# Two interleavings taken out of the compressed attention branch: one product stream after the other, and scores group by group

## What is computed

```
def compress(k, pe, w1, w2):
    blk = k[cmp_idx] + pe[None, :, None, :]
    blk = blk.transpose(0, 2, 1, 3).reshape(n_cmp, G, CMP_BLOCK * dh)
    return jax.nn.silu(blk @ w1) @ w2          # (31, 2, 2048) @ (2048, 256), then @ (256, 64)
k_cmp = compress(kc, pe_k, ck_w1, ck_w2)
v_cmp = compress(vc, pe_v, cv_w1, cv_w2)
sc = jnp.einsum('qghd,cgd->gqhc', qi, k_cmp).astype(jnp.float32) * scale
p_c = jax.nn.softmax(jnp.where(valid[None, :, None, :], sc, NEG), axis=-1)
o_c = jnp.einsum('gqhc,cgd->qghd', p_c.astype(dt), v_cmp)
```

## Time and profile before

| | us |
|---|---|
| median of 3 runs | 2291.12 |
| lowest, highest | 2290.61, 2293.82 |
| the profiled execution (one of the three) | 2293.82 |
| its span in the profile | 2292.0 |
| from the first L1539 to the last VectorE copy of the block | 87.07 to 131.52 |

### The profile page before, as it was taken

One profiled execution on the slowest core, in us unless ns is written; L12 is line 12 of the kernel. 1 busy time (PEld: TensorE's weight loads), 2 busy tenths in 40 slices (PEclk: granted clock), 3 DMA queues, 4 the chain that ended last, 5 costly groups with the idle time before them and its releaser, 6 DMA issues. The chain is left out here.

```text
span 2292.0 us, 26919 instructions
## 1 busy us (share of the span) xinstructions
PE 2137.6 (93%) x10046; PEld 1719.1 (75%) x10046; DVE 1230.9 (54%) x1761; ACT 830.2 (36%) x1204; POOL 18.7 (1%) x46
## 2 busy tenths in 40 slices
PE   7878888999999999998699999999998899999997
PEld 6645666888888888886578888877786577888885
DVE  5576444445443446525567465565535746747465
ACT  4156124433222224224345233343425735424232
POOL 0000000000000000002000000000000000000000
PEclk9889998999999999998799999999999999999998
DMA  4201201322222222221112223221220021232221
GB/s 167 93 1 35 94 28 55 110 101 95 108 92 92 99 96 85 100 89 37 55 61 105 92 94 108 87 97 65 92 94 36 1 88 60 92 111 92 92 96 52
DMA packets 33848, 185.85 MB, mean 81 GB/s; under 512 B 4024, under 2 KB 8280, under 8 KB 14176
## 3 DMA queue, kind: packets, MB, share of 16 engines
q1 hardware_dynamic: 32608, 182.57, 22.7%
q10 hardware_dynamic: 1152, 2.10, 0.3%
HBM read 182.54 MB, written 2.11 MB: 81 GB/s over the span
## 5 line engine op out<-in xcount | busy, mean ns | idle before, releaser
L314 ACT ACTIVATE w_hi<-w_raw 128x2048 fp32r<-128x2048 f32 (+3 forms) x171 | 313.9, 1836 | 846.9 <-PE bank L370 758.8
L368 PE MATMUL bank<-a_hi,w_hi 128*128 128x512 f32 x1488 | 582.8, 392 | 7.0 <-PEq L1442 4.5
L369 PE MATMUL bank<-a_lo,w_hi 128*128 128x512 f32 x1488 | 580.9, 390 | 0.0
L370 PE MATMUL bank<-a_hi,w_lo 128*128 128x512 f32 x1488 | 580.9, 390 | 0.0
L323 DVE TENSOR_TENSOR w_lo<-w_raw,w_hi 128x2048 fp32r<-128x2048 f32 (+3 forms) x171 | 374.8, 2193 | 170.2 <-ACT w_hi L314 170.2
L368 PEld LDWEIGHTS bank<-a_hi,w_hi 128*128 128x128 f32 x1488 | 280.5, 189 | 66.1 <-issue 7.0
L370 PEld LDWEIGHTS bank<-a_hi,w_lo 128*128 128x128 f32 x1488 | 280.4, 188 | 58.7
L369 PEld LDWEIGHTS bank<-a_lo,w_hi 128*128 128x128 f32 x1488 | 280.5, 189 | 57.8
L368 PE MATMUL bank<-big_halves,w_hi 128*128 128x512 f32 x568 | 221.8, 391 | 3.0 <-DVE w_lo L323 3.0
L369 PE MATMUL bank<-big_halves,w_hi 128*128 128x512 f32 x568 | 221.2, 389 | 0.0
L370 PE MATMUL bank<-big_halves,w_lo 128*128 128x512 f32 x568 | 221.1, 389 | 0.0
(11 more groups left out here) (326 smaller groups left out, 2501.0 us busy)
## 6 DMA issues: line engine op xcount, KB each, us to landing
w_raw<-in_w_fu SPq DMA_DIRECT2D x44, 1024.0 KB, 4.8
w_raw<-in_w_up SPq DMA_DIRECT2D x16, 1024.0 KB, 4.8
w_raw<-in_w_down SPq DMA_DIRECT2D x16, 1024.0 KB, 4.8
w_raw<-in_w_fd SPq DMA_DIRECT2D x16, 1024.0 KB, 4.8
w_raw<-in_w_mix SPq DMA_DIRECT2D x8, 1024.0 KB, 4.8
w_raw<-in_w_fd SPq DMA_DIRECT2D x8, 768.0 KB, 4.3
w_raw<-in_w_rqk SPq DMA_DIRECT2D x4, 1024.0 KB, 4.9
w_raw<-in_w_rvg SPq DMA_DIRECT2D x4, 1024.0 KB, 4.8
```

Of the source, the lines that this page charges most:

```text
L314: act.activation(w_hi[slot][:, 0:n], raw[slot][:, 0:n], ACT.Copy).then_inc(hi_ready.sem, 1)
L368: pe.matmul(out, w[0], x[0], start=first, stop=False)
L369: pe.matmul(out, w[0], x[1], start=False, stop=False)
L370: return pe.matmul(out, w[1], x[0], start=False, stop=last)
```

## The change

The lag loop is gone: all 16 matmuls of k (into bank 3) come first, then all 16 of v (into bank 4), both in output partitions 0 to 63, with one signal each. The buffer `hid` becomes 64 partitions by two halves. Silu and the transposes are done once for k and once for v, the transposes with 64 moving columns, into banks 5 and 6. The score loop has the group outermost, and each group's signal comes after its own 16 matmuls. The counts that the engines wait for are moved to fit.

```diff
-            hid = sb(ctx, "cmp_hid", [P, CH])
+            hid = sb(ctx, "cmp_hid", [KV * CB, 2, CH])
...
-                    lag = 6
-                    for n in range(CB // 2 + lag):
-                        for s, j in ((0, n), (1, n - lag)):
-                            if j == 0:
-                                pe.wait_ge(inputs_in[1 + s].sem, loaded[1 + s] + 16)
-                                pe.wait_ge(dve_step.sem, d0 + s + 1)
-                            if 0 <= j < CB // 2:
-                                last = pe.matmul(bank[3][64 * s:64 * s + 64, 0:CH], blk[:, s, j, :, :].rearrange("p g c -> p (g c)"),
-                                                 w1[s][:, j, :], start=j == 0, stop=j == CB // 2 - 1)
-                    last.then_inc(pe_step.sem, 1)
-                    pe.wait_ge(act_step.sem, a0 + 1)
-                    for t in range(2):
-                        last = pe.transpose(bank[5][:, t * P:(t + 1) * P], hid[:, t * P:(t + 1) * P], ident)
-                    last.then_inc(pe_step.sem, 1)
+                    for s in range(2):
+                        pe.wait_ge(inputs_in[1 + s].sem, loaded[1 + s] + 16)
+                        pe.wait_ge(dve_step.sem, d0 + s + 1)
+                        for j in range(CB // 2):
+                            last = pe.matmul(bank[3 + s][0:KV * CB, 0:CH], blk[:, s, j, :, :].rearrange("p g c -> p (g c)"), w1[s][:, j, :],
+                                             start=j == 0, stop=j == CB // 2 - 1)
+                        last.then_inc(pe_step.sem, 1)
+                    for s in range(2):
+                        pe.wait_ge(act_step.sem, a0 + s + 1)
+                        for t in range(2):
+                            last = pe.transpose(bank[5 + s][:, t * 64:(t + 1) * 64], hid[:, s, t * P:(t + 1) * P], ident[0:64, 0:64])
+                        last.then_inc(pe_step.sem, 1)
...
-                    for n in range(4 * TT):
-                        for g in range(KV):
-                            i, h, half = n // 4, n % 4, slice(64 * g, 64 * g + 64)
-                            last = pe.matmul(bank[(2, 7)[g]][:, n * CB:(n + 1) * CB], qk[half, h, i * P:(i + 1) * P], k_cmp[half, :],
-                                             start=True, stop=True)
-                            if n == 4 * TT - 1:
-                                last.then_inc(pe_step.sem, 1)
+                    for g in range(KV):
+                        for i in range(TT):
+                            for h in range(4):
+                                at_col = (i * 4 + h) * CB
+                                last = pe.matmul(bank[(2, 7)[g]][:, at_col:at_col + CB], qk[64 * g:64 * g + 64, h, i * P:(i + 1) * P],
+                                                 k_cmp[64 * g:64 * g + 64, :], start=True, stop=True)
+                        last.then_inc(pe_step.sem, 1)
...
-                    act.wait_ge(pe_step.sem, p0 + 2)
-                    act.activation(hid[:, :], bank[3][:, 0:CH], ACT.Silu).then_inc(act_step.sem, 1)
+                    for s in range(2):
+                        act.wait_ge(pe_step.sem, p0 + 2 + s)
+                        act.activation(hid[:, s, :], bank[3 + s][0:KV * CB, 0:CH], ACT.Silu).then_inc(act_step.sem, 1)
```

More of the change, by code:

```diff
@@ L1543, in _ @@
                     pe.wait_ge(pool_step.sem, g0 + 1)
-                    lag = 6
-                    for n in range(CB // 2 + lag):
-                        for s, j in ((0, n), (1, n - lag)):
-                            if j == 0:
-                                pe.wait_ge(inputs_in[1 + s].sem, loaded[1 + s] + 16)
-                                pe.wait_ge(dve_step.sem, d0 + s + 1)
-                            if 0 <= j < CB // 2:
-                                last = pe.matmul(bank[3][64 * s:64 * s + 64, 0:CH], blk[:, s, j, :, :].rearrange("p g c -> p (g c)"),
-                                                 w1[s][:, j, :], start=j == 0, stop=j == CB // 2 - 1)
-                    last.then_inc(pe_step.sem, 1)
-                    pe.wait_ge(act_step.sem, a0 + 1)
-                    for t in range(2):
-                        last = pe.transpose(bank[5][:, t * P:(t + 1) * P], hid[:, t * P:(t + 1) * P], ident)
-                    last.then_inc(pe_step.sem, 1)
+                    for s in range(2):
[10 more added lines that the diff above has]
+                        last.then_inc(pe_step.sem, 1)
                     pe.wait_ge(inputs_in[3].sem, loaded[3] + 32)
-                    pe.wait_ge(act_step.sem, a0 + 2)
+                    pe.wait_ge(act_step.sem, a0 + 3)
                     for g in range(KV):
@@ L1564, in _ @@
                     last.then_inc(pe_step.sem, 1)
-                    pe.wait_ge(act_step.sem, a0 + 3)
+                    pe.wait_ge(act_step.sem, a0 + 4)
                     for g in range(KV):
@@ L1592, in _ @@
                     act.activation(gate[:, :, :], vg[:, :, 256:280], ACT.Sigmoid)
-                    act.wait_ge(pe_step.sem, p0 + 2)
-                    act.activation(hid[:, :], bank[3][:, 0:CH], ACT.Silu).then_inc(act_step.sem, 1)
-                    act.wait_ge(pe_step.sem, p0 + 3)
-                    turned_hid = bank[5][:, 0:2 * P].rearrange("p (t s g c) -> p t s g c", t=2, s=2, c=CB)
-                    act.activation(hid_k[:, :, :, :], turned_hid[:, :, 0, :, :], ACT.Copy).then_inc(act_step.sem, 1)
+                    for s in range(2):
+                        act.wait_ge(pe_step.sem, p0 + 2 + s)
+                        act.activation(hid[:, s, :], bank[3 + s][0:KV * CB, 0:CH], ACT.Silu).then_inc(act_step.sem, 1)
+                    act.wait_ge(pe_step.sem, p0 + 4)
+                    act.activation(hid_k[:, :, :, :], bank[5][:, 0:P].rearrange("p (t g c) -> p t g c", t=2, c=CB), ACT.Copy).then_inc(act_step.sem, 1)
+                    act.wait_ge(pe_step.sem, p0 + 5)
                     for h in range(4):
-                        last = act.activation(hid_v[:, :, :, h, :], turned_hid[:, :, 1, :, :], ACT.Copy)
+                        last = act.activation(hid_v[:, :, :, h, :], bank[6][:, 0:P].rearrange("p (t g c) -> p t g c", t=2, c=CB), ACT.Copy)
                     last.then_inc(act_step.sem, 1)
@@ L1620, in _ @@
                         last.then_inc(dve_step.sem, 1)
-                    dve.wait_ge(pe_step.sem, p0 + 4)
+                    dve.wait_ge(pe_step.sem, p0 + 6)
                     dve.tensor_copy(k_cmp[:, :], bank[0][:, 0:CB]).then_inc(dve_step.sem, 1)
-                    dve.wait_ge(pe_step.sem, p0 + 5)
+                    dve.wait_ge(pe_step.sem, p0 + 7)
                     dve.wait_ge(pool_step.sem, g0 + 2)
@@ L1630, in _ @@
                     for g in range(KV):
-                        dve.wait_ge(pe_step.sem, p0 + 6 + g)
+                        dve.wait_ge(pe_step.sem, p0 + 8 + g)
                         s4 = bank[(2, 7)[g]][:, :].rearrange("p (i h c) -> p i h c", h=4, c=CB)
@@ L1639, in _ @@
                     for g in range(KV):
-                        dve.wait_ge(act_step.sem, a0 + 4 + g)
+                        dve.wait_ge(act_step.sem, a0 + 5 + g)
                         dve.tensor_reduce(mx[:, g, :, :], sc[:, g, :, :, :], AX_X, ALU.add)
@@ L1652, in _ @@
                     for g in range(KV):
-                        dve.wait_ge(pe_step.sem, p0 + 8 + g)
+                        dve.wait_ge(pe_step.sem, p0 + 10 + g)
                         dve.tensor_copy(probs_t[:, g, :], bank[3 + g][:, :]).then_inc(dve_step.sem, 1)
                     for h in range(4):
-                        dve.wait_ge(pe_step.sem, p0 + 10 + h)
+                        dve.wait_ge(pe_step.sem, p0 + 12 + h)
                         dve.tensor_copy(o[:, h, :], bank[4 + h][:, :])
-            pe_step.n += 13
+            pe_step.n += 15
             dve_step.n += 10
-            act_step.n += 5
+            act_step.n += 6
             pool_step.n += 2
```

## The result

| | before | after |
|---|---|---|
| first comparison, 4 runs each: median | 2292.31 | 2304.16 |
| ratio (95% interval) | | 1.0054 (1.0042 to 1.0067) |
| second comparison, 29 and 6 runs | 2296.65 | 2304.24, ratio 1.0038 (1.0025 to 1.0051) |
| third comparison, 18 and 7 runs | 2296.52 | 2304.45, ratio 1.0030 (1.0019 to 1.0041) |
| span of the profiled execution | 2292.0 | 2302.2 |

The change makes the kernel slower, in all three comparisons by more than the measurement is uncertain: +12.4, +8.7 and +6.9 us by the ratios. (A ratio is an estimate of its own and not the quotient of the two medians, which differ by 11.9, 7.6 and 7.9 us.) The kernel's own spread is wide (2288 to 2301 us for the kernel before over all sessions), and the four runs of before in the first comparison lay low. The forecast was +9.9 us, a ratio of 1.0043.

What follows compares the result with a forecast made beforehand. TensorE was busy 93% of the span, but the changed stage was read as a serial chain between engines. Stream and handover +4.8 us and unpaired scores +5.1 made +9.9, forecast 2301.0 us, range 2294.0 to 2304.5.

Steps and rivals of the forecast that it cites:

- step 4: Small products before the scores: the clock falls near 112.2, some three of L1568's eight passes are slow, +0.3 us.
- step 5: Scores by group, unpaired, all at half clock: group 1 ready at 126.8 instead of 116.9, +9.9 us with the earlier steps.
- step 6: Everything after the scores shifts as it stands: nothing added, 2 us kept for where the clock changes.
- steps 1 and 5: Lone passes: first stream 0.215 us each at full clock, +4.7 us; score loads 0.111 us full, 0.213 half clock.
- steps 2 and 3: Silu in two halves adds nothing; four smaller transposes let hid_v wait for the v ones alone, -0.2 us.
- the first rival: The clock falls one stretch later, at about 115.6, within the scores: +7.1 us, 2298.2 us, chance 0.17.
- The early signal: Group 0's softmax runs under group 1's scores, saving 2.14 us.
- full clock through the scores: Clock stays full in the score products: +3.2 us, 2294.3 us, chance 0.06.
- half-priced loads: A lone score load costs half of a pair, 0.107 us at half clock: +3.3 us, 2294.4 us, chance 0.06.
- the cold stream: The lone first stream does not raise the clock: +21.5 us, 2312.6 us, chance 0.04.
- the clock kept to the next stage: The fuller stream keeps the clock up from the scores until the next stage: -2.8 us, 2288.3 us, chance 0.04.
- added load times: In the scores, load and moving columns add in one row group, 0.267 us a pass: +13.3 us, 2304.4 us, chance 0.03.

Runs made afterwards that it cites:

- c2_after: The changed kernel, with no further edit, run and profiled a second time; ratio 1.0038 to the kernel before.
- e6_delay6: The kernel before with 8 extra VectorE copies ahead of group 0's bias addition, no product changed; ratio 1.0031, +7.1 us.
- e2_groups: The kernel before with only the scores taken group by group, each group with its own signal, first stream unchanged; ratio 1.0021, +4.8 us.

## Why the prediction came out as it did

The direction and the size of the whole held: +9.9 forecast, +6.9 to +12.4 measured. But the range ended at 2304.5: the median of 2304.16 lies just inside, and 1.0054 on that comparison's 2292.31, 2304.7, just above it. The parts held less well than the sum. Two steps failed, step 4 (the clock, and through it step 5) and step 6 (nothing outside the stage), with errors of opposite sign; that the whole came so near was luck.

- **The price of a pass, steps 1 and 5: right.** 0.215 lone and paired at full clock in the stream, 0.11 and 0.21 for a lone score load. The stream's last pass in c2_after starts 16.2 us after the first, as worked out.
- **The handover, steps 2 and 3: right.** From the last stream pass to the first score it takes 3.1 us in c2_after (109.65 to 112.75) against 3.4 before; forecast was -0.2.
- **Step 4, the clock, failed.** The forecast had the clock fall near 112.2, ahead of the scores. It fell at 115.7, 115.8 and 116.2 in the three profiles. That was the first rival, with +7.1 us and a chance of 0.17. I gave it too little: I put the fall at the like place, behind the small products with their idle time, although in the new kernel that stretch begins with the last microsecond of the stream. Whether that is what kept the clock up no run shows.
- **Step 5's sum, as a result, was 3.8 us too high.** Group 1's softmax starts 29.65 us after the stream's start in c2_after and 23.58 before: +6.1, not +9.9. 28 passes at full clock that were priced at half make 2.9 us of it. Four of group 1's passes ran beside group 0's, 0.85 us, a term that the forecast didn't have. The rival's +7.1 less these 0.85 is +6.2.
- **Step 6, "I add nothing", was too low.** Outside the stage the changed kernel's three profiles have 4.3 to 5.0 us more than the first profile of before (the first 1.8 ahead of the stage and 3.2 in the rest, the others 4.5 in the attention) and 1.6 to 2.2 more than the second profile of before, which itself has 2.8 more attention. A pure delay, e6_delay6, shows the same 90.2 us of attention, so in that block it is not the change's products. That it is where the work lies among the stretches of the granted clock fits the profiles, 2.8 of the 4.4 us by the rows of L1128; the 3.2 us in the rest of the first profile no run explains. I had kept 2 us for all of this, and single executions differ by more: outside the stage e2_groups has 2.3 us less than the first profile of before. By the ratios of the second and third comparison what lies outside the stage is 0.7 to 3.5 us. Part of the 12.4 of the first comparison is also that its runs of before were low: 1.0038 and 1.0030 came from 29 and 18 runs.
- **The early signal, right:** 2.13 us of the 2.14.
- **The other rivals:** full clock through the scores, half-priced loads, the cold stream, the clock kept to the next stage and added load times were not seen in any profile of the changed kernel. The forecast's chances for the three cases within 0.2% add to 0.16, not 0.15.

## What to carry to other kernels

Products that use half of the array's rows or columns are worth ordering by halves, alternating from one to the next: each pair costs one here. An early signal for half of the work must be set against what the grouping takes from the pairs; here it gave back 2.1 us of 6. In a stage that is all handovers, price every step at both levels of the clock, and keep a few microseconds of the range for where the clock changes, ahead of the stage and behind it too.

## What the runs showed of the hardware beyond that

- TensorE starts loads of the next group beside the last ones of the present group if they lie in the other row half: four of them, 0.85 us (e2_groups and c2_after).
- One kernel's executions differ by where the granted clock changes. Ahead of the stage the clock was half for 3.4 us in the kernel before (78.1 to 81.5) and for 6.8 in the changed one (78.1 to 85.0), over identical instructions, and the stage started 1.8 us later. The changed kernel's other two profiles have 3.4 us there again, so it is not the change.
- Products whose result nobody reads, put in TensorE's waits, kept the clock full over the first stream and made the kernel 6 us faster (0.9973), though they held the first transposes back by about 1 us.
